# Full-precision products of 512 columns written as four products of 128 columns

## The reference, cut to what matters

```python
sc = jnp.einsum('bqkgd,bskd->bkgqs', qblk, k).astype(jnp.float32)
p = jax.nn.softmax(sc, axis=-1).astype(v.dtype)
```

```python
w_log = -jax.nn.softplus(-(w0 + jnp.tanh(wd) @ w2)) - 0.5
decay = jnp.exp(-jnp.exp(w_log.astype(f32)))
a = jax.nn.sigmoid(a0 + ad @ a2)
g = jax.nn.sigmoid(gd) @ g2
...
bonus = jnp.sum(r_h * k_h * r_k.astype(f32), axis=-1, keepdims=True) * v_h
```

## Time and profile before

| what | value |
|---|---|
| median of 3 runs | 2902.47 us (2902.18 to 2905.0) |
| the profiled execution | 2902.36 us |
| its span, first to last instruction | 2900.2 us |
| PE busy | 2703.2 us, 93% of the span |
| DVE busy | 2068.0 us, 71% |
| ACT busy | 1272.6 us, 44% |
| POOL busy | 890.6 us, 31% |
| mean granted clock of PE | 0.972 |

### The profile page before, as it was taken

The page is one execution under the profiler, slowest core; times in us unless marked ns, Lnnn a source line. Parts: engine busy times, 40 slices in busy tenths (PEclk is TensorE's granted clock), DMA queues, the critical chain, the costliest instruction groups (busy, mean ns, idle before and its releaser), DMA issues. The chain is left out here.

```text
span 2900.2 us, 54410 instructions
## 1 busy us (share of the span) xinstructions
PE 2703.2 (93%) x21301; PEld 1682.7 (58%) x21301; DVE 2068.0 (71%) x3800; ACT 1272.6 (44%) x2187; POOL 890.6 (31%) x606
## 2 busy tenths in 40 slices
PE   8898999978999999999979999978989989999998
PEld 4454465555677777777754646654666664444443
DVE  6564289998788888888876447765677764777742
ACT  4674243478333333333342137754555543433321
POOL 0772444500555555555520132213322221000000
PEclk9998999999999999999989899989999999999999
DMA  4005644576999999999953231114111125622321
GB/s 150 30 1 203 212 134 147 180 262 269 383 381 362 360 362 364 362 364 364 356 176 92 88 113 56 54 48 144 37 42 55 37 71 183 216 88 87 116 80 52
DMA packets 278539, 513.29 MB, mean 177 GB/s; under 512 B 19472, under 2 KB 166544, under 8 KB 276432
## 3 DMA queue, kind: packets, MB, share of 16 engines
q1 hardware_dynamic: 241488, 376.48, 38.0%
q0 software_dynamic: 36864, 134.23, 11.9%
HBM read 445.05 MB, written 65.60 MB: 176 GB/s over the span
## 5 line engine op out<-in xcount | busy, mean ns | idle before, releaser
L1894 PE MATMUL banks<-gated_hi,v_lo 128*128 128x384 bf16 (+2 forms) x1536 | 335.1, 273 | 0.0
L1894 PE MATMUL banks<-gated_lo,v_hi 128*128 128x384 bf16 (+2 forms) x1536 | 335.1, 273 | 0.0
L1894 PE MATMUL banks<-gated_hi,v_hi 128*128 128x384 bf16 (+2 forms) x1536 | 335.1, 273 | 0.0
L1732 POOL DMA_INDIRECT gathered_u<-in_u_rows,first_tile_rows x128 | 212.2, 1658 | 298.7 <-DVE gathered_dots L1840 156.3
L1737 POOL DMA_INDIRECT gathered_v<-in_v,first_tile_rows x128 | 175.4, 1370 | 201.9 <-DVE x_tokens L1832 182.1
L1894 PEld LDWEIGHTS banks<-gated_hi,v_hi 128*128 128x128 bf16 x1536 | 150.1, 98 | 56.3 <-issue 0.8
L1881 PE MATMUL banks<-act_hi,u_hi 128*128 128x384 bf16 x512 | 168.0, 328 | 12.0 <-DVE u_lo L1818 12.0
L1802 ACT CAST gated_hi<-gated 128x384 bf16<-128x384 f32 x128 | 65.5, 512 | 254.6 <-DVE gated L1854 254.6
L1832 DVE SCALAR_TENSOR_TENSOR x_tokens<-gathered_v,gathered_weights,x_tokens 128x1024 f32<-128x1024 f32 x128 | 164.0, 1281 | 6.2 <-DVE gathered_weights L1823 3.0
L1881 PE MATMUL banks<-act_lo,u_hi 128*128 128x384 bf16 x512 | 167.9, 328 | 0.0
L1252 PE MATMUL banks<-act_hi,early_u_hi 128*128 128x384 bf16 x512 | 167.9, 328 | 0.0
(11 more groups left out here) (628 smaller groups left out, 7403.6 us busy)
## 6 DMA issues: line engine op xcount, KB each, us to landing
shared_room<-in_u SPq DMA_DIRECT2D x128, 512.0 KB, 7.7
shared_hi<-in_v SPq DMA_DIRECT2D x64, 512.0 KB, 13.2
shared_lo<-in_v SPq DMA_DIRECT2D x64, 512.0 KB, 5.4
gate_tables<-gate_piece SPq DMA_DIRECT2D x12, 2048.0 KB, 8.6
gate_group<-gate_tables SPq DMA_DIRECT2D x32, 768.0 KB, 10.3
late_raw<-in_ffn_up SPq DMA_DIRECT2D x22, 1024.0 KB, 7.6
early_gelu<-early_gelu_columns SPq DMA_DIRECT2D x64, 192.0 KB, 1.9
gelu_early_rows<-early_gelu SPq DMA_DIRECT2D x32, 384.0 KB, 11.9
```

Source lines behind the costliest of these rows:

```text
L1732: pool.indirect_dma_start(gu[:, n % GROUP, :], None, u_table, bass.IndirectOffsetOnAxis(ap=rows.index[:, 0, n:n + 1], axis=0)).then_inc(gu ...
L1894: m = pe.matmul(ps[:, bank, to:to + width], v[:, j, cols], w[:, j, tok:tok + width], start=start and n == 0 and to == 0, stop=stop and n = ...
```

## The change

Every float32 product of 512 moving columns is written as four products of 128 columns with the same weights. For `gate`, where two products add up, each quarter of the columns gets both before the next quarter begins. The signal to the waiting engine stays on the last product.

```diff
-                    pe.matmul(ps[:, u % 2, :], qT[lo:lo + HD, h // 2, t * P:(t + 1) * P],
-                              kT[lo:lo + HD, h // 4, :], start=True, stop=True).then_inc(scored, 1)
+                    for s in range(NT):
+                        cols = slice(s * P, (s + 1) * P)
+                        last = pe.matmul(ps[:, u % 2, cols], qT[lo:lo + HD, h // 2, t * P:(t + 1) * P],
+                                         kT[lo:lo + HD, h // 4, cols], start=True, stop=True)
+                    last.then_inc(scored, 1)
...
+                def by_columns(w, x):
+                    for c in range(NCH):
+                        cols = slice(c * P, (c + 1) * P)
+                        ins = pe.matmul(ps[:, SMALL, cols], w, x[:, cols], start=True, stop=True)
+                    return ins
...
-                    pe.matmul(ps[:, SMALL, :], wj2[:, j % 2, 1, :], low_z[:, 1, :], start=True, stop=False)
-                    rest(pe.matmul(ps[:, SMALL, :], wj2[0:32, j % 2, 2, :], low_z[0:32, 2, :], start=False, stop=True), "gate")
+                    for c in range(NCH):
+                        cols = slice(c * P, (c + 1) * P)
+                        pe.matmul(ps[:, SMALL, cols], wj2[:, j % 2, 1, :], low_z[:, 1, cols], start=True, stop=False)
+                        ins = pe.matmul(ps[:, SMALL, cols], wj2[0:32, j % 2, 2, :], low_z[0:32, 2, cols], start=False, stop=True)
+                    rest(ins, "gate")
...
-                    rest(pe.matmul(ps[:, SMALL, :], ones_rk[:], rk, start=True, stop=True), "bonus")
+                    rest(by_columns(ones_rk[:], rk), "bonus")
...
-                    first(pe.matmul(ps[:, SMALL, :], wj2[0:64, j % 2, 0, :], low_z[0:64, 0, :], start=True, stop=True), "decay_in")
+                    first(by_columns(wj2[0:64, j % 2, 0, :], low_z[0:64, 0, :]), "decay_in")
...
-                    first(pe.matmul(ps[:, SMALL, :], wj2[64:128, j % 2, 0, :], low_z[64:128, 0, :], start=True, stop=True), "rate_in")
+                    first(by_columns(wj2[64:128, j % 2, 0, :], low_z[64:128, 0, :]), "rate_in")
```

## The result

| | before | after |
|---|---|---|
| median of the runs | 2903.73 us (8 runs, 2899.72 to 2908.74) | 2915.73 us (8 runs, 2910.19 to 2924.92) |
| ratio, with its 95% interval | | 1.0045 [1.0034, 1.0056] |
| the profiled execution | 2902.36 us | 2915.49 us |
| its span | 2900.2 us | 2913.3 us |
| mean granted clock of PE | 0.972 | 0.972 |

What follows compares the result with a forecast made beforehand. PE was taken to bound the kernel, busy 2703.2 of 2900.2 us; `gate` 9.4 + `bonus` 0.3 + 64-row products 1.9 = 11.6 us on 2902.36 gave 2914.0 us, range over all cases 2907 to 2918.

Steps and rivals of the forecast that it cites:

- The split of the 1.05 us: One float32 product of 512 columns between other row counts: 0.10 uncovered load, two streams of 0.43, 0.09 gap.
- the piece of 0.41: Each of eight pieces in `gate`: 0.10 load, two records of 0.11, 0.09 gap; +1.17 us a `gate`, +9.4 us in all.
- The upper bound: In `gate`, second load not beside the first stream: 0.52 us a piece, `gate` 4.16 us, +16.4 us in all.
- the lower (0.22): In `gate`, row count changes cost nothing: 0.22 us a piece, `gate` 1.95 us, -1.3 us in all.
- Is it on the path?: `gate` heads each pass's serial chain, so the chain through `bonus` to `lx` moves back by the same 1.2 us.
- the rival by which a pass's waits take up the longer `gate`: PE's 4.5 us of waits per pass hide half or all of the 9.4: 2909.3 or 2904.6 us; chance 0.08.
- 64 rows and `bonus`: `score`, `decay_in`, `rate_in`: +0.04 us for each of 48 products, +1.9 us; `bonus`: +0.04, eight times, +0.3 us.
- The first rival: Row count changes inside `gate` cost nothing, next load beside the running stream; kernel not slower, 2903.3 us; chance 0.08.
- The clock: Rival: clock falls behind every `gate`, 1.6 us each, 2926.8 us; one or two falls, 2916 to 2917; chance 0.07.

## Why the prediction was right, step by step

**The split of the 1.05 us, and the piece of 0.41.** Right. The pieces stand 0.41 to 0.42 us apart, and `gate` takes 3.33 us where 3.28 was forecast: +1.22 instead of +1.17. The upper bound (loads and streams in turn, 0.52) and the lower (0.22) both fell in the first trace, and with all pieces on 128 rows the lower one is what a piece costs.

**"Is it on the path?"** Yes. A pass without a fall is longer by 1.30 to 1.33 us, of which `gate` gives 1.22. The rest of the chain moved back with it; the timeline of DVE and the first `lx` of the changed kernel, beside the earlier trace rows:

```profile
2249.43 0.69 DVE L2715 TENSOR_TENSOR low_t_masked<-low_t,level_masks 128x1024 bf16<-128x1024 bf16 x1
2251.41 0.69 DVE L2674 TENSOR_TENSOR bonus<-banks,z_pair 128x512 f32<-128x512 f32 x1 [1.29 <-PE banks L3184]
2253.54 1.36 DVE L2721 TENSOR_TENSOR inverses<-banks,inverses 128x512 bf16<-128x512 f32 x2
```

```profile
2254.37 0.40 PE L3331 MATMUL banks<-inverses,low_t_masked 128*128 128x64 bf16 x8 [0.16 <-DVE inverses L2721]
```

DVE, which stood still for 0.03 us ahead of `bonus`'s reader, now waits 1.29 us for PE there, and `lx` still waits for DVE, 0.16 us. So the rival by which a pass's waits take up the longer `gate` is false. The small +0.19 of pass 1 looks like it, but is a fall of the clock that went away.

**64 rows and `bonus`.** The sizes are right in the trace, a unit of the attention +0.03 and `bonus` +0.02, where 0.04 was forecast for each; `decay_in` and `rate_in` were not read apart, but with them the sizes fit the 0.1 us that a pass has beside `gate`. The 1.3 us forecast for the attention, though, can't be found at its end. The first `low_gram` starts 0.07 us earlier than before, and over the kernels run here it starts anywhere from 1977.7 to 1987.5 us: what lies between the attention and the recurrence varies by more than this term.

**The first rival** (changes of row count cost nothing) is false: with one change, or none, the pieces take 2.17 and 1.89 us, and the kernel is as fast as before.

**The clock** is the step that was judged too low. The rival had 0.07 with the argument that PE has pauses of 0.2 us, no idle. The rival's own case was a fall behind every `gate`, which didn't come; one or two falls, worth 1.6 us each, lay in its range. Three came, worth 1.3 to 1.4 each, less one of before that vanished: +3 us net. That the total is only 1.5 us above the forecast is partly luck: the passes without a fall came out as summed (1.29 us each forecast, 1.30 to 1.33 measured), and +3 of the clock stand against 1.3 us of the attention that don't appear.

## What to carry to other kernels

Before splitting a product or setting two side by side, compare their row counts: each change of the row count between neighbouring float32 products here cost some 0.2 us, a load that nothing covers and a gap. Beside bf16 products it was less: the two changes around a `score` cost 0.22 us together (3.244 against 3.026 us a unit). So group by row count, or fill up with zero rows to 128. Such rows cost PE no time here (a record streams for 0.43 us either way), and the version with them was 10.7 us faster than the kernel before, though its rows account for only some 7 of them. And the chain that PE heads here passed on the whole of the cost, although 4.5 us of each pass are waits of PE.

## What the runs showed of the hardware that was not expected

The granted clock fell to 1.2 GHz right behind, or in the last 0.2 us of, a stretch in which PE's records leave no gap, 3.3 us of pieces with alternating row counts. It did so behind 3, 3, 2 and 2 of eight `gate`s in the four traces with such pieces, inside all eight with the pieces twice, and behind none in the seven kernels without them (the one before among them, each with one trace). The only other `gate` with a fall is the first one of the kernel all on 128 rows, where it begins 0.6 us into the `gate`, soon after a wait of PE of 1.65 us for DVE that every kernel has there. Between a `gate` with a fall and one without, no row shows a difference. A piece whose records last 0.49 us and start 0.41 us after those of the last one reads as a busy PE, yet it streams for only 2 x 0.11 us: a busy share from records says little of what the array does.
